# An encoder block's expert stage: gates placed in DRAM by adding indirect DMAs, low parts of the keys moved to VectorE

## The reference, cut to what matters

```python
def peer_ffn(x, w_query, sub_keys, expert_u, expert_v):
    qry = (t @ w_query).reshape(nt, PEER_HEADS, 2, PEER_QDIM // 2)
    s = jnp.einsum('thzd,hzkd->thzk', qry, sub_keys)
    top_s, top_i = lax.top_k(s, PEER_TOPK)
    cand_s = (top_s[:, :, 0, :, None] + top_s[:, :, 1, None, :]).reshape(nt, PEER_HEADS, kk)
    cand_i = (top_i[:, :, 0, :, None] * PEER_KEYS + top_i[:, :, 1, None, :]).reshape(nt, PEER_HEADS, kk)
    best_s, best_pos = lax.top_k(cand_s, PEER_TOPK)
    idx = jnp.take_along_axis(cand_i, best_pos, axis=-1)
    gate = jax.nn.softmax(best_s, axis=-1)
    act = jax.nn.gelu(jnp.einsum('td,thkd->thk', tb, expert_u[ib]), approximate=False)
    return jnp.einsum('thk,thkd->td', act * gate, expert_v[ib])
```

## Time and profile before

| | us |
|---|---|
| Runs | 2757.78, 2761.29, 2764.63 (median 2761.29) |
| Profiled execution, its own time | 2742.67 |
| Its span, first to last instruction | 2740.9 |
| of which the up stage | 1210 to 2086 |
| of which the down stage | 2086 to 2652 |

### The profile page before, as it was taken

One profiled execution on the slowest core, in us unless ns is written; L12 is line 12 of the kernel. 1 busy time (PEld: TensorE's weight loads), 2 busy tenths in 40 slices (PEclk: granted clock), 3 DMA queues, 4 the chain that ended last, 5 costly groups with the idle time before them and its releaser, 6 DMA issues. The chain is left out here.

```text
span 2740.9 us, 35437 instructions
## 1 busy us (share of the span) xinstructions
PE 2495.9 (91%) x11629; PEld 2025.9 (74%) x11629; DVE 1658.4 (61%) x2562; ACT 959.5 (35%) x1340; POOL 1463.7 (53%) x893
## 2 busy tenths in 40 slices
PE   7998887888699997989899999999997999999977
PEld 5886476777678886877787777778775788887765
DVE  4333566777642122145798489389404999999842
ACT  5444212333333222313452443354233333333322
POOL 3442254666543342424664574475446888888841
PEclk9999767899899998999999999999998999999989
DMA  3220000000022221314338336434765999999930
GB/s 143 92 92 31 1 0 6 1 0 0 31 94 91 93 92 59 110 39 138 100 103 243 115 98 208 149 102 146 237 216 201 344 350 346 345 347 336 332 133 31
DMA packets 175499, 383.26 MB, mean 140 GB/s; under 512 B 18128, under 2 KB 100176, under 8 KB 167632
## 3 DMA queue, kind: packets, MB, share of 16 engines
q1 hardware_dynamic: 152912, 315.32, 34.0%
q0 software_dynamic: 22528, 67.19, 7.3%
HBM read 321.63 MB, written 60.82 MB: 140 GB/s over the span
## 5 line engine op out<-in xcount | busy, mean ns | idle before, releaser
L1400 POOL TENSOR_TENSOR up_u_low_sb<-up_u_sb,up_u_high_sb 128x1024 fp32r<-128x1024 f32 x128 | 328.9, 2570 | 415.9 <-ACT up_u_high_sb L1505 415.9
L173 PE MATMUL ps<-n_high_sb,up_u_high_sb 128*128 128x512 f32 x1024 | 413.5, 404 | 23.0 <-POOL up_u_low_sb L1400 22.8
L174 PE MATMUL ps<-n_low_sb,up_u_high_sb 128*128 128x512 f32 x1024 | 407.1, 398 | 0.0
L175 PE MATMUL ps<-n_high_sb,up_u_low_sb 128*128 128x512 f32 x1024 | 407.1, 398 | 0.0
L1754 PE MATMUL ps<-down_v_high_sb,down_w_high_sb 128*128 128x512 f32 x768 | 302.7, 394 | 28.7 <-POOL down_v_low_sb L1677 28.5
L1755 PE MATMUL ps<-down_v_low_sb,down_w_high_sb 128*128 128x512 f32 x768 | 300.0, 391 | 0.0
L1756 PE MATMUL ps<-down_v_high_sb,down_w_low_sb 128*128 128x512 f32 x768 | 299.9, 391 | 0.0
L173 PEld LDWEIGHTS ps<-n_high_sb,up_u_high_sb 128*128 128x128 f32 x1024 | 195.1, 191 | 77.0 <-POOL up_u_low_sb L1400 34.6
L1651 ACT ACTIVATE down_v_high_sb<-down_v_sb 128x1024 fp32r<-128x1024 f32 x128 | 125.0, 1048 | 351.1 <-PE ps L1756 337.0
L1006 POOL TENSOR_TENSOR merge_low_sb<-merge_slots_sb,merge_high_sb 128x2048 fp32r<-128x2048 f32 x28 | 129.3, 4620 | 221.2 <-ACT merge_high_sb L1000 221.2
L175 PEld LDWEIGHTS ps<-n_high_sb,up_u_low_sb 128*128 128x128 f32 x1024 | 194.6, 190 | 46.1
(11 more groups left out here) (315 smaller groups left out, 5657.2 us busy)
## 6 DMA issues: line engine op xcount, KB each, us to landing
up_u_sb<-expert_u SPq DMA_DIRECT2D x128, 512.0 KB
down_v_sb<-expert_v SPq DMA_DIRECT2D x128, 512.0 KB
a_dense<-up_gelu_sb SPq DMA_DIRECT2D x128, 256.0 KB
g_dense<-up_gates_sb SPq DMA_DIRECT2D x24, 1024.0 KB
down_gelu_sb<-a_dense SPq DMA_DIRECT2D x128, 192.0 KB
down_gates_sb<-g_dense SPq DMA_DIRECT2D x128, 192.0 KB
w_slots_sb<-w_conv SPq DMA_DIRECT2D x20, 1024.0 KB, 4.8
merge_slots_sb<-w_gates SPq DMA_DIRECT2D x16, 1024.0 KB
```

The costliest lines, as they stand in the source:

```text
L173: pe.matmul(out, ah, bh, start=k == 0, stop=False)
L174: pe.matmul(out, ah, bl, start=False, stop=False)
L175: last = pe.matmul(out, al, bh, start=False, stop=k == n - 1)
L1400: pool.tensor_tensor(ul[:, n, :, :], u[:, n, :, :], bits32(uh[:, n, :, :]), ALU.subtract).then_inc(low, 1)
```

## The change

**Placing.** The one-hot matmuls, their one-hots, the transposes, the copies to `up_gates` and the 24 stores of 1 MB go. VectorE works out for each chosen pair the cell of `g_dense` that it belongs to (`place`), and GpSimd issues for each dense tile 128 indirect DMAs. Each takes one gate of each of the 128 tokens from SBUF (4 bytes each) and adds it to its cell in DRAM. Before each further head (16 of these DMAs) GpSimd waits until all those of the heads before have landed. So that there is something to add to, `g_dense` (25 MB) is cleared in the gdn stage: GpSimd makes a tile of zeros before its first wait there, and SP stores it eight times, 3.1 MB each, and waits for them before that stage's barrier.

**Keys.** `up_u`, its parts and the gelu have four buffers (`RING`). GpSimd makes the low parts of keys 0 to 11 only (`FIRST`), VectorE those of keys 12 to 127. In VectorE's program one low part is set behind every 4.2 us of selection (`PACE`), by an estimate for each step that is written in the code, starting from -62 us; what is left of them stands behind the last tile. ACT's exponential of a tile stands three keys ahead of the key that VectorE has come to.

**SP.** The loads of V for the down stage come with keys 100 to 107. The loads of its first gelus and gates (16 DMAs) stand behind all keys, behind a wait for all adding DMAs and a wait for the last gelu stores, and ahead of the stage's barrier.

```diff
+                    if h:
+                        pool.wait_ge(added[tt], 16 * TOPK * h)
+                    for k in range(h * TOPK, (h + 1) * TOPK):
+                        at = bass.IndirectOffsetOnAxis(ap=place[:, tt, k:k + 1], axis=0)
+                        pool.indirect_dma_start(cells, at, gates[:, tt, k:k + 1], None, compute_op=ALU.add).then_inc(added[tt], 16)
...
+            sp.wait_ge(nought_made, 1)
+            for j in range(0, PEER_K, CLEAR):
+                sp.dma_start(m.g_dense[j:j + CLEAR].rearrange("j i t -> i j t"),
+                             nought[:, :].unsqueeze(1).broadcast_to([P, CLEAR, TD])).then_inc(cleared, 16)
+            sp.wait_ge(cleared, 16 * (PEER_K // CLEAR))
...
+            for tt in range(DENSE):
+                sp.wait_ge(added[tt], 16 * HK)
+            for n in range(RING):
+                sp.wait_ge(a_stored[n], 16 * (BLOCKS + 1))
+            for b in range(2):
+                for j in range(DOWN_J):
+                    down.load_weights(sp, b, b, j)
...
+            split = [FIRST, -62.0]
+
+            def low_part():
+                j, n = split[0], split[0] % RING
+                dve.wait_ge(high, j + 1)
+                dve.tensor_tensor(ul[:, n, :, :], u[:, n, :, :], bits32(uh[:, n, :, :]), ALU.subtract).then_inc(low_dve, 1)
+                split[0] += 1
+
+            def spent(us):
+
+                split[1] += us
+                if split[1] >= PACE and split[0] < PEER_K:
+                    split[1] -= PACE
+                    low_part()
...
+                st.done(dve.scalar_tensor_tensor(at_f[:, :], second, float(P), first, ALU.mult, ALU.add))
+                st.done(dve.scalar_tensor_tensor(at_f[:, :], at_f[:, :], float(TD if tt < DENSE else T),
+                                                 token[:, tt:tt + 1].broadcast_to([P, HK]), ALU.mult, ALU.add))
+                if tt < DENSE:
+                    dve.tensor_copy(place[:, tt, :], at_f[:, :]).then_inc(placed, 1)
```

More of the change, by code:

```diff
@@ L741, in gdn_stage @@
     dve_s, halves_in = m.sem("gdn_dve_steps"), m.sem("gdn_halves_loaded")
+    nought = work.take("nought", [P, TD])
+    cleared, nought_made = m.sem("gate_cells_cleared"), m.sem("nought_made")
+    CLEAR = 16
     bank = lambda u, n: m.ps[:, 2 * u + n, :]
@@ L1327, in up_stage @@
     best, pos, part = take("best", [P, PEER_H, TOPK]), take("pos", [P, PEER_H, TOPK], U32), take("part", [P, HK], U32)
-    part_f, sums = take("part_f", [P, HK]), take("sums", [P, PEER_H])
-    chosen = take("chosen", [P, 3, HK])
-    high_t = take("chosen_t", [P, 3, P])
-    gate_h, gate_l = take("gate_high", [P, P], F32R), take("gate_low", [P, P])
-    hot_i, hot_h, hot_l = (take(f"hot_{x}", [P, STEP, P], F32R) for x in ("first", "high", "low"))
-    r = m.region(AT_END - KB_GATES, AT_END)
-    gs = take("gates", [P, PEER_K, P])
@@ L1342, in up_stage @@
-    high, low, prod, gelu = sem("u_high_done"), sem("u_low_done"), sem("products"), sem("gelu_done")
+    part_f, sums, token = take("part_f", [P, HK]), take("sums", [P, PEER_H]), take("token", [P, TT])
+    chosen, at_f = take("chosen", [P, 2, HK]), take("place", [P, HK])
+    gates, place = take("gates", [P, DENSE, HK]), take("gate_at", [P, DENSE, HK], U32)
+    sem = lambda name: m.sem(f"up_{name}")
+    dve_s, exped, placed, maxed = (sem(x) for x in ("dve_steps", "gate_exp", "gates_placed", "best_less_max"))
@@ new lines, in _ @@
+        @block.gpsimd
+        def _(pool):
+            for j in range(FIRST):
+                n = j % RING
+                pool.wait_ge(high, j + 1)
+                pool.tensor_tensor(ul[:, n, :, :], u[:, n, :, :], bits32(uh[:, n, :, :]), ALU.subtract).then_inc(low_pool, 1)
+            for tt in range(DENSE):
+                pool.wait_ge(placed, tt + 1)
+                for h in range(PEER_H):
+                    if h:
[3 more added lines that the diff above has]
+                        pool.indirect_dma_start(cells, at, gates[:, tt, k:k + 1], None, compute_op=ALU.add).then_inc(added[tt], 16)
@@ L1498, in _, with split @@
         @block.scalar
         def _(act):
-            act.sem_inc(gs_done, FOURS)
-            act.sem_inc(gelu, 2)
-            def split(j, n):
-                act.wait_ge(u_in[n], j * 8 + (16 - 8 * n))
+            act.sem_inc(gelu, RING)
+            def split(j):
+                n = j % RING
+                act.wait_ge(u_in[n], 16 * (j // RING + 1))
                 act.activation(uh[:, n, :, :], u[:, n, :, :], ACT.Copy).then_inc(high, 1)
-            def key(j, n, more=True):
+            for n in range(RING):
+                split(n)
@@ L1509, in key @@
+            for j in range(PEER_K):
+                for tt in range(TT):
+                    if j == max(exp_at[tt] - RING + 1, 0):
+                        gate = gates[:, tt, :] if tt < DENSE else m.v_gate[:, tt - DENSE, :]
+                        act.wait_ge(maxed, tt + 1)
+                        act.activation(gate, gate, ACT.Exp).then_inc(exped, 1)
+                n = j % RING
                 act.wait_ge(prod, j + 1)
-                act.wait_ge(a_stored[n], j * 8 + (16 - 8 * n))
+                act.wait_ge(a_stored[n], 16 * (j // RING + 1))
@@ L1581, in _ @@
-            with pe.Fori(0, TAIL // 2) as i:
-                for n in range(2):
-                    key(i * 2 + (PEER_K - TAIL + n), n)
+            with pe.Fori(0, FIRST // RING) as i:
+                for n in range(RING):
+                    pe.wait_ge(low_pool, i * RING + (n + 1))
+                    key(n, i * RING + (n + 1))
+            with pe.Fori(0, BLOCKS - FIRST // RING) as i:
+                for n in range(RING):
+                    pe.wait_ge(low_dve, i * RING + (n + 1))
+                    key(n, i * RING + (FIRST + n + 1))
```

245 lines of the change are left out of this document (66 added, 179 removed).

## The result

The changed kernel takes 3059.7 us (median of 4 runs, 3053.23 to 3069.14) against 2759.53 us of the kernel before (4 runs on the same chip, 2750.9 to 2764.63). The ratio is 1.109, with a 95% interval of 1.105 to 1.114: 11% slower, where 5% faster was forecast. The profiled execution is the one of 3053.23 us, with a span of 3051.4. Against the profiled execution before (2742.67) that is 310.6 us more.

The account below looks back on a forecast made before the run. It took TensorE to bound the up stage: -141.1 us there and +8.8 us of loads at the stage's end gave -132.3, other terms nothing, so 2629.0 us from a median of 2761.29; range 2605 to 2730.

Parts of the forecast that it names:

- TensorE and the removed one-hots: Up stage: without 768 one-hot matmuls and their waits TensorE ends at 1940.6 instead of 2081.7, -141.1 us.
- Low parts on VectorE: Up stage: 116 low parts at 1.212 us, 141 us on VectorE, which keeps ahead of TensorE; cost nothing.
- Clearing: Gdn stage: 25.2 MB of zeros stored to DRAM while the DMA engines are nearly idle; cost 0.
- The end of the stage: Up stage's end: SP issues sixteen loads between the last store's landing and the barrier, +8.8 us.
- The rest of the down stage: Down stage behind its first matmul: nothing else changes, no cost.
- The adding DMAs: GpSimd's chain in the up stage: starts at 1278, ends at 1920, 23 us before SP needs it; costs nothing.
- 384 x 1.49 = 572: GpSimd's issue of all adds, priced by a 4-byte gather's mean 1.189 us plus a 0.30 us gap: 572 us.
- the landing between heads: GpSimd's 21 waits for the head before and the last landing, 3.2 us each: 70 us.
- the adds throttle GpSimd: Rival: slow DMA engines fill the queue and GpSimd issues at their pace; slower than before, break-even 1.89 us per DMA; chance 0.15.
- fixed 2.0 us: Throttling rival's estimate from the skill's page: completion paid per DMA in line, 384 x 2.0 + 70 = 838, total 2802 us.
- the slower rival's own bound of 2917: Throttling rival at the longest gather's 2.30 us per DMA: chain ends at 2231, 288 us late, total 2917 us.

Follow-up runs that it names:

- one tile of adds: Changed kernel with only the first tile's 128 adding DMAs issued, the other two tiles' gates left out: 2613.96 us, ratio 0.951 to the kernel before.
- the kernel with alternating adds: Changed kernel, adding DMAs and 1024 bytes, with heads of two tiles alternating from the fifth head on: 3007.96 us, one run.
- the alternating kernel: Kernel with VectorE-summed gates, plain scatters and 2048 bytes, heads reordered so two tiles alternate from the fifth: first 2643.77 to 2737.47 us, rerun median 2641.36.

## Why the prediction was wrong, point by point

**TensorE and the removed one-hots: right.** The forecast had TensorE done with the keys at 1940.6. Its last key matmul starts at 1932.3, and it waits for low parts only at the start, 8.7 us. The keys' matmuls took 715.4 us instead of 864.1, so TensorE lost 149 us where 141.1 were forecast; the 7.6 us more are not explained.

**Low parts on VectorE: right.** 116 of 1.223 us, and VectorE waits for ScalarE's high parts (311 us), TensorE never for VectorE. What I didn't count is what they do to GpSimd: long adds.

**Clearing: right, cost nothing.** The first key matmul of the up stage is where it was (1217.1 us, 1217.6 before), and the gdn window moves 97 GB/s at a share of 0.27.

**The end of the stage: right.** With one tile of adds SyncE waits 1.6 us for the gelu store, and the down stage's first matmul (1959.3) comes 26 us behind the last key's (1933.2); 27 were forecast.

**The rest of the down stage: wrong, a term put at nothing.** "Nothing else of the down stage changes", but from its first matmul to its last it takes 559.5 us where it took 541.4. Its 4-byte gathers take GpSimd 187.0 us instead of 152.2, and TensorE's waits for GpSimd's low parts inside the stage grow from 10.2 to 24.3 us. In the kernel with alternating adds it is 542.6 us and 159.1 us of gathers. Why the same gathers take longer in most of the changed kernels was not looked into.

**The adding DMAs: wrong, and this is nearly the whole error.** The step that failed is "384 x 1.49 = 572". I took 1.49 us a DMA from the gather, and bounded it at 2.30 by the longest gather. It was (629.6 + 413.6) / 384 = 2.72, beyond the bound. Two terms were missing or too small. The duration is 1.640 instead of 1.189 on average, 173 us, of which the median alone (1.556 against the gather's 0.952) says that the adding form costs 0.6 us. And the waits for room, 305 us in 153 gaps, had no term at all. The term that I did fear, the landing between heads, was put at 22 x 3.2 = 70 us; the 21 waits took 48.9, and the last landing 3.2. The sum of the chain was 642 and is 1092; it ends 435 us after SyncE would have gone on, and 435 - 132 = 303 of the measured 310.6 us follow. Behind the 8 us left are mostly two larger ones, 18 more in the down stage and 7.6 less in the keys.

**Where the argument broke.** The rival "the adds throttle GpSimd" had the right sign and the break-even (1.89 us), and got 0.15. I argued it down with packets: four gathers took 96 (in truth three did) at 12 ns of engine time each, "so even ten times that is 1 us". But the packets per DMA were not what counts: an add makes 144 of them, and an engine is still idle 84% of the time. The rival's mechanism was wrong as well: the queue doesn't fill because the engines are slow. What limits is neither engine, but the room: each time it is used up, GpSimd waits for the landing of the DMA that it has just issued. The trace of before couldn't show that: no gap between two of its gathers is longer than 0.31 us, and they come in groups of eight with other work between. The line with `dynamic_dma_scratch_size=1024` stood in the kernel and I costed nothing by it. The Trainium skill's fixed 2.0 us, mostly completion, cited there, gave 2802 by an estimate that paid it for every DMA. The landing measured 3.0 us, and it was paid 153 + 21 times and not 384; with 2048 bytes the adds' mean step of 2.18 us behind TensorE is near 2.0 only by accident of the room.

**The range** reached to 2730 and left out the slower rival's own bound of 2917, which itself fell 140 us short. A bound from the nearest row isn't a bound when the operation differs in kind (here: it reads, adds and writes) and when it is repeated 384 times in a row where the row's own came eight at a time.

## What to carry to other kernels

Before many small indirect DMAs replace other work, ask what room their descriptors have and after how many of them it is used up, and count a wait for a landing each time; that few are in flight at once doesn't help, and a price from a short burst says nothing of a long series. Scatter where the data can be made to allow it, rather than add: summing duplicates on an engine with time to spare cost 165 us of VectorE off the path, and saved 370 us of the kernel's time with 1024 bytes of room and 191 with 2048. And a chain on another engine is free until it ends behind the one that bounds the stage; from there every microsecond of it counts in full, so its slack (23 us here, on 642) has to be weighed against how well its price is known.

## What the runs showed of the hardware

- A 128-element indirect DMA of 4 bytes each takes GpSimd 0.96 us to write when it scatters, and 1.556 when it adds; it makes 32 and 144 packets.
- With 512, 1024 and 2048 bytes of room, 362, 153 and 51 of 383 steps between adding DMAs held a wait for room (nearly every one, two in five, every seventh). The mean step where nothing else runs, waits for the head before included, is 3.51, 2.57 and 2.18 us. Plain scatters waited at every seventh with 1024 bytes and at every 14th with 2048.
- Such a wait ends 0.39 to 0.59 us after the landing of the DMA issued last (1024 bytes, all 153), and its place depends on the number of DMAs issued since the tile's first, not on what is in flight.
- From issue to landing an add takes 3.0 us (median) with the DMA engines otherwise idle, 3.9 (1024 bytes) and 5.0 us (512 bytes) beside the loads of the up stage.
- In an execution of the alternating kernel TensorE's matmuls stood up to 2.80 us apart, where 0.233 is usual, between 1690 and 1848 us, with nothing in the kernel that they waited for. The granted clock was 0.97 from 1600 to 1700 us and 0.50, the 1.2 GHz level, from 1750 to 1830:

```profile
1747.16 0.59 PE L174 MATMUL ps<-n_high_sb,up_u_high_sb 128*128 128x512 f32 x1 [2.21 <-issue]
1749.96 0.59 PE L175 MATMUL ps<-n_low_sb,up_u_high_sb 128*128 128x512 f32 x1 [2.21 <-issue]
1752.76 0.59 PE L176 MATMUL ps<-n_high_sb,up_u_low_sb 128*128 128x512 f32 x1 [2.21 <-issue]
```

Its cause stays open.
